# Hybrid decoder step on one core: operands of the second output pair moved, first value tiles reordered, block pieces loaded first

## What is computed

```python
xn = rmsnorm(x, norm_w)
q, k, v, i_pre, f_pre, o_pre, z_m, b_g, c_g, x_c, z_c, g_m, g_c = split(xn @ w_in)
h, C1, n1, m1 = mlstm_chunkwise(q, k, v, ig, lf, C0, n0, m0)
h = rms(h) * head_norm_w * sigmoid(o_pre) * silu(z_m)
y_m = h @ w_proj_m
cv, conv1 = short_conv(c_g * x_c, conv0, conv_w)
y_c = (silu(z_c) * b_g * cv) @ w_proj_c
mix = sigmoid(g_m) * y_m + sigmoid(g_c) * y_c
out = x + mix @ w_out            # then a final rmsnorm with final_norm_w
```

## Time and profile before

| what | value |
|---|---|
| median of 3 runs | 2289.41 us (2287.56 to 2292.71) |
| profiled execution | 2289.31 us, of which the span is 2287.6 us |
| TensorE busy | 2253.8 us, 99% of the span |
| VectorE, ScalarE, GpSimd busy | 1687.4 us (74%), 1059.2 us (46%), 158.9 us (7%) |
| granted TensorE clock, mean | 0.998 |
| DMA | 469.38 MB, 205 GB/s on the mean |

### The profile page before, as it was taken

How to read it: one execution, slowest core, us unless ns; L and a number is a source line. 1 busy time by engine, 2 the same in 40 slices (tenths; PEclk the granted TensorE clock), 3 DMA queues, 4 the chain that set the end, 5 groups by cost and what they waited for, 6 DMA issues and landing times.

```text
span 2287.6 us, 41437 instructions
## 1 busy us (share of the span) xinstructions
PE 2253.8 (99%) x14531; PEld 2189.7 (96%) x14531; DVE 1687.4 (74%) x2951; ACT 1059.2 (46%) x1961; POOL 158.9 (7%) x136
## 2 busy tenths in 40 slices
PE   8999999999999999999999999999999999999998
PEld 8998999999999999999999999999999999998886
DVE  4447789998787588877767578777776867766775
ACT  3224455344455455455656455555565524323432
POOL 0011122100012100100001000100000000011000
PEclk9999999999999999999999999999999999999999
DMA  6674778655787767755584767575576757769643
GB/s 229 203 234 127 247 243 262 191 179 176 227 269 228 250 209 237 232 175 181 185 255 162 220 206 229 163 222 174 182 230 186 222 185 248 203 153 249 164 159 112
DMA packets 477760, 469.38 MB, mean 205 GB/s; under 512 B 36410, under 2 KB 390842, under 8 KB 477622
## 3 DMA queue, kind: packets, MB, share of 16 engines
q1 hardware_dynamic: 466358, 446.50, 62.4%
q0 software_dynamic: 4352, 8.46, 2.4%
q10 hardware_dynamic: 6912, 12.59, 1.6%
HBM read 319.48 MB, written 148.01 MB: 204 GB/s over the span
## 4 chain that ended last, share of the span: by engine, by line
PE 78%; issue 5%; DVE 3%; DMA 2%; POOL 1%; SPq 1%; ACT 1%; ACTq 0%; POOLq 0%; DVEq 0%
PE b_g L1915 53%; PE c_g L2500 12%; PE c_g L2524 7%; PE b_n L1970 1%; PE b_s L1968 1%; PE b_n L1969 1%; DVE x_lo L1549 1%; PE b_s L1952 1%; PE b_t L1974 1%; DMA proj_whole<-sums_d 1%; DMA h<-w_proj_c 1%; POOL h L1313 0%; SPq L1044 0%; POOL neg_max L1321 0%; POOL h L1316 0%
## 5 line engine op out<-in xcount | busy, mean ns | idle before, releaser
L1915 PE MATMUL b_g<-x_hi,w_hi 128*128 128x344 f32 (+1 forms) x3024 | 983.5, 325 | 10.1 <-DVEq L1514 2.7
L1915 PE MATMUL b_g<-x_lo,w_hi 128*128 128x344 f32 (+1 forms) x3024 | 966.4, 320 | 0.0
L1915 PE MATMUL b_g<-x_hi,w_lo 128*128 128x344 f32 (+1 forms) x3024 | 965.3, 319 | 0.0
L1915 PEld LDWEIGHTS b_g<-x_hi,w_hi 128*128 128x128 f32 x3024 | 568.3, 188 | 16.5 <-issue 6.9
L1915 PEld LDWEIGHTS b_g<-x_lo,w_hi 128*128 128x128 f32 x3024 | 568.2, 188 | 1.7
L1915 PEld LDWEIGHTS b_g<-x_hi,w_lo 128*128 128x128 f32 x3024 | 568.2, 188 | 0.0
L1371 ACT ACTIVATE w_hi<-w_operands 128x512 fp32r<-128x512 f32 x519 | 324.6, 628 | 308.8 <-PE b_g L1915 252.7
L1528 DVE TENSOR_TENSOR w_lo<-w_operands,w_hi 128x512 fp32r<-128x512 f32 x519 | 368.7, 720 | 10.9 <-ACT w_hi L1371 8.9
L2500 PE MATMUL c_g<-act_hi_a,proj_ops 128*128 128x258 f32 x1024 | 187.2, 283 | 1.7 <-PEq L989 1.7
L1371 ACT ACTIVATE w_hi<-stages 128x512 fp32r<-128x512 f32 x216 | 134.3, 628 | 110.4 <-PE b_g L1915 108.7
L2500 PEld LDWEIGHTS c_g<-act_hi_a,proj_ops 128*128 128x128 f32 x1024 | 158.8, 189 | 2.2 <-DVE proj_ops L257 2.2
(11 more groups left out here) (315 smaller groups left out, 3046.8 us busy)
## 6 DMA issues: line engine op xcount, KB each, us to landing
w_operands<-w_in SPq DMA_DIRECT2D x282, 256.0 KB, 5.2
stages<-w_ops_d SPq DMA_DIRECT2D x36, 768.0 KB, 4.8
w_operands<-w_ops_d SPq DMA_DIRECT2D x34, 768.0 KB, 4.9
stages<-w_in SPq DMA_DIRECT2D x72, 256.0 KB, 3.3
w_operands<-w_ops_d SPq DMA_DIRECT2D x70, 256.0 KB, 6.2
w_ops_d<-w_operands SPq DMA_DIRECT2D x18, 768.0 KB, 3.7
w_ops_d<-stages SPq DMA_DIRECT2D x18, 768.0 KB, 3.4
proj_whole<-sums_d SPq DMA_DIRECT2D x46, 256.0 KB, 5.9
```

Of the source, the lines that this page charges most:

```text
L1915: last = nc.tensor.matmul(bank[:, 0:n], w[:, j, k, :], x[:, k, 0:n], start=(j < 4 and k == 0 and m == 0), stop=(k == 3 and m == 2), skip_g ...
```

## The change

What it does, part by part:

- Value stage. SyncE issues the row load of tile 4 at i = 2, ahead of store_x(0), and not at i = 3. The load of 1 MB of weights for the next stage goes from i = 2 to i = 6. ScalarE splits tile 3 (hi(3)) ahead of the loop; in body 3 the square of tile 4 stands behind the evacuation. VectorE does variance(2) and lo(3) ahead of norm(0) and norm(1); in body 3 variance(4) stands behind the evacuation.
- Projection stage. In SyncE's body, load_weights stands directly behind load_w of the first pair, ahead of the chunk's loads, the row and operand stores and load_quarters.
- Branch stage, u = 1. act_sum(1) is done at product 1, and not at product 0.
- End of the branch stage and output stage. load_mix(1) is issued behind the whole weights of pair 5. While pair i = 0 runs, everything that splits the rows of pair 1 is done three products later (behind_first); the last three act_high and the last four act_low stand behind the loop over j.

```diff
             for i in range(2, NT):
-                if rows(i) == P:
+                if rows(i) == P and i != 3:
                     load_x(i + 1, 1 - i % 2)
                 if i == 2:
+                    load_x(4, 0)
                     store_x(0, 0)
...
+                if i == 6:
+                    load_blocks(sp, g, 0, COL["q"], COL["k"], w0_in)
                 if i == 2:
-                    load_blocks(sp, g, 0, COL["q"], COL["k"], w0_in)
                     store(0, 0)
...
             square(2, 0)
+            hi(3, 1)
...
-                if not second:
+                if not second and not third:
                     hi(i, par)
+                if rows(i) == P and not third:
+                    square(i + 1, 1 - par)
                 if rows(i) == P:
-                    square(i + 1, 1 - par)
                     diagonal(i, par)
...
                 if not second:
                     evac(i - 1, 1 - par)
+                if third:
+                    square(i + 1, 1 - par)
...
             evac(1, 1)
+            variance(2, 0)
+            lo(3, 1)
             norm(0, 0)
             norm(1, 1)
-            variance(2, 0)
...
-                if rows(i) == P:
+                if rows(i) == P and not third:
                     variance(i + 1, 1 - par)
-                if second:
-                    lo(3, 1)
-                else:
+                if not second:
                     evac(i - 1, 1 - par)
+                if third:
+                    variance(i + 1, 1 - par)
...
                 if following:
                     load_w(pair + 2, *following, 0)
+                if block_of(p, s, i) is not None:
+                    load_weights(block_of(p, s, i))
...
-                if block_of(p, s, i) is not None:
-                    load_weights(block_of(p, s, i))
...
+    def behind_first(i):
+
+        return 3 if i == 0 else 0
...
-                if u >= NU - 2:
-                    load_mix(u - NU + 2)
+                if u == NU - 2:
+                    load_mix(0)
                 if u in (6, 7, 14, 15):
                     for j in range(NOP):
                         load_pair({6: 2, 7: 3, 14: 4, 15: 5}[u], j)
+            load_mix(1)
...
-                    if i + 1 < NT2:
-                        act_high(nc, act, g, S0 + i + 1, j)
+                    if i + 1 < NT2 and j >= behind_first(i):
+                        act_high(nc, act, g, S0 + i + 1, j - behind_first(i))
...
+                for j in range(NOP - behind_first(i), NOP):
+                    act_high(nc, act, g, S0 + i + 1, j)
...
-                    if u == 1 and j == 0:
-                        act_sum(nc, dve, g, s, 0)
-                        act_sum(nc, dve, g, s, 1)
+                    if u == 1 and j < 2:
+                        act_sum(nc, dve, g, s, j)
...
-                    if i + 1 < NT2:
-                        if j == 0:
+                    if i + 1 < NT2 and j >= behind_first(i):
+                        at = j - behind_first(i)
+                        if at == 0:
...
-                            act_low(nc, dve, g, s, j - 1)
-                            if j < 3:
-                                act_sum(nc, dve, g, s, j + 1)
+                            act_low(nc, dve, g, s, at - 1)
+                            if at < 3:
+                                act_sum(nc, dve, g, s, at + 1)
...
-                    act_low(nc, dve, g, s, NOP - 1)
+                    for j in range(NOP - 1 - behind_first(i), NOP):
+                        act_low(nc, dve, g, s, j)
```

More of the change, by code:

```diff
@@ L595, in _ @@
             square(2, 0)
+            hi(3, 1)
             def body(i, par):
                 second = isinstance(i, int) and i == 2
-                if not second:
+                third = isinstance(i, int) and i == 3
+                if not second and not third:
                     hi(i, par)
+                if rows(i) == P and not third:
+                    square(i + 1, 1 - par)
                 if rows(i) == P:
-                    square(i + 1, 1 - par)
                     diagonal(i, par)
```

## The result

The changed kernel takes 2275.60 us, the median of six runs (2270.44 to 2278.11), against 2288.36 us of the kernel before (six runs, 2287.56 to 2292.71). The ratio is 0.9935, 95% interval 0.9925 to 0.9945. Forecast was 2275.7, in a range of 2270.5 to 2282. Measured again later the ratio was 0.9940 (0.9927 to 0.9954). The profiled execution took 2274.59 us with a span of 2272.9; the kernel before had 2289.31 and 2287.6.

A forecast was written before the change was run, and what follows sets the result against it. TensorE was taken to be busy for all but some 34 us, so only shortening its waits could pay. Terms -4.6 - 3.1 + 1.1 - 7.0 = -13.6 took 2289.3 to 2275.7 us, range 2270.5 to 2282.

The forecast's parts named there:

- Value stage, 4.6 forecast: Value stage, tiles 2 to 4: earlier variance, low part and row load remove waits of 0.57, 1.72 and 2.33 us; 4.6 saved.
- Early pieces, 3.1 forecast: Projection stage, block sums: loading raw weight pieces earlier saves 5.46 - 0.3 - 2.0 = 3.1 us, between 5.5 and 0.5.
- The +2.0 at the turn: Turn of the pass, block 8: earlier GpSimd work slows VectorE's last x_lo and first weight splits; 2.0 us slower, bounds 0 and 3.5.
- The 3.29 at block 6: Block 6: TensorE's 3.29 us wait in three pieces, behind ScalarE standing until GpSimd is done, goes.
- The rest that I put at 0.3 in block 0: Block sums, mainly block 0: 0.3 us taken off the saving for GpSimd work now beside other VectorE work.
- u = 1, +1.1 forecast: Branch stage, u = 1: moving sum 1 removes a 1.14 us wait but delays act_high and later splits; 1.1 us slower.
- End, 7.0 forecast: Start of output stage: pair 5's weights issued earlier remove a 5.41 us wait and 2.1 us of slow clock; 7.0 saved.
- The residual of 0.5: Start of output stage: 0.5 us left for a load that lands later because the queue is no emptier.
- The first (the late load changes its name): Rival, output stage: pair 5's weights or mix(1) still land late; the end saves 3, not 7; 2279.7 us, chance 0.22.
- the third (the order doesn't bind): Rival: block loads still wait in a full DMA queue, tile 4 still stalls; only 7.0 less 1.1 saved; 2283.4, chance 0.09.
- The second, that no new stall comes: Rival: all stalls go and the new ones at block 8 and u = 1 don't come; 18.7 saved, 2270.6, chance 0.15.
- The fourth, GpSimd against VectorE in every body: Rival: GpSimd's subtractions exclude VectorE in every pass body, 12 x 2.0 = 24 us lost against 16; 2297.3, chance 0.04.

## Why the prediction was right, point by point

- **Value stage, 4.6 forecast.** The three waits went as reckoned, undone they came back (0.57, 1.72, 2.24), worth some 5.6 us in time. Tile 4 was not late, nor tiles 7 to 9: the moved 1 MB load made no wait.
- **Early pieces, 3.1 forecast.** Undone it costs some 4.2 us in time; TensorE's waits from 300 to 720 us are 5.4 without it and 3.5 and 2.5 in the two profiles of the changed kernel. Three terms were mis-sized, in ways that nearly cancelled.
  - The +2.0 at the turn measured 0.67 (1.08 against 0.41) in six of seven profiles with the early place. That GpSimd would begin on top of the last x_lo was right: it began while the second one ran. But then the x_lo kept its time, and only one stretched weight split, not two operations, stood ahead of what TensorE waited for. In the seventh profile an x_lo lost 1.10 as well, and the cost was 1.75.
  - The 3.29 at block 6 didn't all go. The prediction put its three pieces down to ScalarE, but the first, 1.45, hung on VectorE's wait of 6.11 us for an operand. In the nine profiles with the early place at block 6 ScalarE's pieces are gone; VectorE's wait for that load is still 4.2 to 7.0 us, and TensorE's behind it 0 to 1.8.
  - I had no term for block 7: its wait of 0.6 to 1.5 us comes with the early pieces (in six of seven profiles with them, in none of four without). That the sums' stores, now beside the operand loads, make them late is argued from the issue times only; not tested by itself. The rest that I put at 0.3 in block 0 showed instead as 0 to 1.1 at block 5, where VectorE's work beside GpSimd was stretched.
  - The lower bound of this part was given as 0.5; its own terms give 5.46 - 0.3 - 3.5 = 1.7. Nothing hung on it.
- **u = 1, +1.1 forecast.** Between the two profiles it had the wrong sign: a wait of 0.80 in place of 1.14. The experiments show the mechanism right: with the weight equally early, the moved sum costs 0.7 to 1.3 us of wait (seven profiles) and the old order none (two profiles). Of the two delays that the prediction named, only the second, at product 6, shows in the changed kernel. The first, of 1.2 a product earlier, hung on a weight as late as in the execution I had read, and here the weight landed 2 us earlier; where it came later again (27.6 us, the run with sums 2 and 3 moved), there were 0.73 us at product 5.
- **End, 7.0 forecast.** 7.2 between the two profiles. With the rows loaded first the wait was 5.41, 2.95 and 5.66 us in three profiles, and the execution before had one of the long ones; the times give 5.4 and 6.5. The residual of 0.5 is fair: 0 to 1.3 us, at a later product, in the profiles with the new order. In the three profiles with the rows loaded first the slow clock went with the wait, as in the earlier trace rows, and they agree with the Trainium skill's rule on an idle TensorE ("TensorE: Matmul & The Clock Gate", Part 1, What's actually happening). The 2.87 us wait of the run with the order alone, followed by a clock of 1.00, does not; what decided it stays open.
- **Rivals.** The first (the late load changes its name) and the third (the order doesn't bind) are refuted by the profiles of the end and of block 6 and tile 4; the times alone would not exclude the first. The second, that no new stall comes, is refuted by the waits at the turn and in u = 1. The fourth, GpSimd against VectorE in every body, is not seen: none of blocks 9 to 11 made a wait. The Trainium skill's rule that it drew on ("SBUF — State Buffer", Who interferes with whom) holds in the trace (1.35 against 0.68 beside GpSimd). The price that the prediction worked out from it for block 8, 3.5, is twice to five times what was measured (1.75 and 0.67): what VectorE loses costs only what its slack doesn't hold.
- **Signs.** Those for the value stage and for the first output matmul came true. Three didn't: a wait stands behind block 5 (1.08); the wait of u = 1 moved two products later and not one; and a sign of being wrong, a weight split stretched beside GpSimd where TensorE then waits, is there at the turn and at block 5. It cost 0.67 and up to 1.1 us, too little to turn the result.

That the total came within 0.1 us is partly luck. Cut at TensorE's first matmul of the passes and at the first and the last one of the branch stage, the profile of after is shorter than that of before by 3.3, 3.2, 1.0 and 7.2 us, where the forecast had 4.6, 3.1, -1.1 and 7.0. In each of the first two stretches it holds a slow stretch of some 1.5 us that no term foresaw (below); without these two the profile would be 17.7 us shorter, where 13.6 were forecast. In the branch stage the term had the wrong sign because of the earlier weight.

## What to carry to other kernels

When TensorE is 99% busy, its list of waits, with the slow stretches behind them, is nearly the whole budget: follow each wait back to the instruction that stands ahead of the late one in a written order, and move that. Moving a load later needs its consumers moved as well, or they block everything queued behind them; here neither half alone gave a gain that the time can tell. A term read from one profile is one draw of the DMA queues: the landing of a weight moved by 2 us between executions and turned the sign of what one edit seemed to do.

## What was not expected of the hardware

Executions of one kernel differ by 2 to 9 us here, and the profiles show part of it. At the end of the value stage TensorE waits 2.7 us in every profile. In the one of the kernel before the clock stayed at 1.00 afterwards; in that of the changed kernel, and in all nine others, it was granted less for 3 to 6 us. First the kernel before, then the changed one:

```profile
215.00:220.00 5.00, 4.99 (x31) 5.00 (x32) 3.74 (x4) 5.00 (x6) 4.53 (x9) 1.00 0.58 221
```

```profile
211.69:216.00 4.31, 4.31 (x18) 4.31 (x19) 3.09 (x2) 3.37 (x5) 4.24 (x8) 0.60 0.58 221
```

By the spacing of the matmuls (0.29 us against 0.16) that costs 1.3 to 2.6 us. Behind the wait of 1.3 to 3.5 us at the kernel's start the same happened in five of eleven profiles, at 1.3 to 1.5 us each, and not in order of length: not behind 3.48, but behind 1.99. At the end it was the same: a clock of 0.50 behind a wait of 2.95 us and of 1.00 behind one of 2.87. So equal waits are not followed by equal clocks, and a forecast from one profile carries some 3 us of it. What decides it is open.
